# First two weight-block sums of 25 seven-product pairs: by DMAs that add in SBUF instead of one VectorE instruction each

## The chip, the cores and the metric

One core of a Trainium2 chip runs the whole kernel. The metric is the device time of one execution, in microseconds (us). The engines are named as in the profile: PE is TensorE's matmuls, PEld its weight loads, DVE is VectorE, ACT is ScalarE, POOL is GpSimd, and SP is SyncE, which here issues DMAs only (SPq is its queue).

## The reference

A decoder layer for 256 tokens of width 2048: a projection, two kinds of attention, an output projection with layer norm, and then the MLP, which is all that matters here:

```python
hdn = jnp.square(jax.nn.relu(jnp.einsum('bsd,df->bsf', x, w_ff1[l])))
ff_out = jnp.einsum('bsf,fd->bsd', hdn, w_ff2[l])
x = layer_norm(DEEPNORM_ALPHA * x + ff_out, ln2_g[l], ln2_b[l])
```

x is 256 x 2048, w_ff1 is 2048 x 8192 and w_ff2 is 8192 x 2048, all float32.

## The kernel before

**Three products for one.** Each float32 operand is split in a rounded part (hi, written by ScalarE as fp32r) and the rest (lo, written by VectorE as the difference). A product is then made as three matmuls: hi x hi, hi x lo, lo x hi (the helper `three`, L808 to L810).

**Parts and passes.** The 8192 hidden columns are worked in two parts, chunks 0 to 6 and 7 to 15 (`FF_PARTS`). In a part the hidden values of its chunks are made first (w_ff1). Then two passes over its rows of w_ff2 follow, one for each half (1024) of the output columns. So there are four passes: 0 and 1 from about 553 to 697 us, 2 and 3 from about 897 to 1082 us, with the hidden stage of part 1 between them.

**Pairs.** A pass goes over pairs of 128-row tiles of w_ff2, numbered through all passes as q (64 pairs; `PAIRS`). A pair's weights are a 2 x 2 grid of blocks of 128 x 512: tile t or t + 1, left or right 512 of the columns. There are two kinds. A plain pair (37 of them) makes the 8 block products of 2 tiles, 2 token halves and 2 column halves, 24 matmuls of 512 columns. A seven-product pair (27, `FAST`) makes 7 products, as in Strassen's and Winograd's scheme, 21 matmuls, from sums of weight blocks (`sum_raw`, four blocks) and from three of the blocks themselves ("own"), against sums of hidden blocks made earlier. The two kinds alternate, seven-product pair first, until the seven-product pairs of the pass are through; some plain pairs come at the end of a pass (3 in most). `NTH` counts the pairs of a kind.

**The steps of a seven-product pair q.** SyncE loads 1 MB into one of three buffers in two DMAs (`load_pair`, L490) once the pair that had the buffer before (q - 3) is split. VectorE makes the sums (`sum_pair`): first two blocks in one instruction of 1024 elements (L1640: block 1 + block 0 and block 2 + block 0), then the third from the first (L1647), then the fourth from the third (L1650), 512 each. ScalarE rounds the first two, then the last two (`round_sums`, L1188, L1190) and the own blocks (`round_own`, L1201). VectorE splits the first two, the last two (`split_sums`, L1659) and the own blocks (`split_own`, L1666). TensorE (`fast_group`) waits for the first split, multiplies with sums 0 and 1, then waits for the second and third split. sum_raw and sum_lo are one buffer; sum_raw, sum_hi and the own blocks exist once, so a step for the next pair waits until TensorE has used them (`fast_used`, counted three times in a pair).

**Plain pairs.** ScalarE rounds in two pieces of 1024 (L1181) and VectorE splits in two (L1631), in one of two homes.

**Order.** Each engine's order is written out by hand: pair after pair, for VectorE sums, splits, own, then the next plain pair. At the end of passes 0 and 2 (`end_pass`) it is: drain the low banks, sums of the next pass's first pair, split of the last plain pair, splits of those sums. GpSimd has no work in the passes: it waits for the final norm. The seven-product pairs 0 and 30 (`PART_END + 2`) are the first ones of each part; pair 30's sums are made before its part's plain pairs.

Of the kernel before, what the change touches and what calls it, by code (L numbers as in the profile page):

```python
# [4 lines left out]
P = 128  # L5
F32 = mybir.dt.float32
F32R = mybir.dt.float32r
ALU = mybir.AluOpType
ACT = mybir.ActivationFunctionType
# [9 lines left out]
NC = 512  # L19
CHUNKS = D_MODEL // NC  # L20
CHUNKS_FF = D_FF // NC
KU = 2
SLOTS = 4
UPH = KT // KU
# [4 lines left out]
U_FF1 = U_OUT + UPH * CHUNKS  # L29
# [44 lines left out]
HALF = D_MODEL // 2  # L74
# [18 lines left out]
PASSES = [(part, half) for part in range(2) for half in range(2)]  # L93
PAIRS = [(p, t) for p, (part, half) in enumerate(PASSES) for t, fast in pass_order(part, half)]
FAST = [fast for part, half in PASSES for t, fast in pass_order(part, half)]
PASS_START = [min(q for q, (of, t) in enumerate(PAIRS) if of == p) for p in range(len(PASSES))]
PASS_END = [max(q for q, (of, t) in enumerate(PAIRS) if of == p) + 1 for p in range(len(PASSES))]
NTH = [FAST[:q].count(FAST[q]) for q in range(len(PAIRS))]
FAST_END = [FAST[:end].count(True) for end in PASS_END]
PLAIN_END = [end - fast for end, fast in zip(PASS_END, FAST_END)]  # L100
PART_END = PASS_END[1]
# [10 lines left out]
STORE_ORDER = [0, 1, 2, 7, 3, 4, 5, 8]  # L112
BY_SCALAR = [6]

LAMBDA_INIT = 0.8 - 0.6
EPS = 1e-5
ALPHA = 2.0 ** 0.25
# [43 lines left out]
def hybrid_layer(nc, x, x_turned, w_in, lq1, lk1, lq2, lk2, subln_g, w_out, ln1_g, ln1_b, w_ff1, w_ff2,  # L161
# [3 lines left out]
    KB = 1024  # L165

    def at(name, shape, dtype, offset):
        return nc.alloc_sbuf_tensor_at(name, shape, dtype, offset=base + offset)
# [12 lines left out]
    X0 = 55 * KB  # L181
# [3 lines left out]
    H0 = X0 + 32 * KB  # L185
# [29 lines left out]
    E0 = H0 + 121 * KB  # L215
    sum_raw = at("sum_raw", [P, 4 * NC], F32, E0)
    sum_lo = at("sum_lo", [P, 4 * NC], F32R, E0)
    sum_hi = at("sum_hi", [P, 4 * NC], F32R, H0 + 97 * KB)
    last_hi = at("last_hi", [P, 4 * NC], F32R, X0 + 20 * KB)
    last_lo = at("last_lo", [P, 4 * NC], F32R, H0 + 16 * KB)  # L220
    last_raw = at("last_raw", [P, 4 * NC], F32, H0 + 24 * KB)
# [47 lines left out]
    def sem(name):  # L269
        sems[name] = nc.alloc_semaphore(name)  # L270
        return sems[name]
# [7 lines left out]
    w_rounded, w_split, w_used = sem("w_rounded"), sem("w_split"), sem("w_used")  # L279
# [26 lines left out]
    pair_loaded = [sem(f"pair_loaded{s}") for s in range(4)]  # L306
    plain_rounded, plain_split, plain_used = sem("plain_rounded"), sem("plain_split"), sem("plain_used")
    fast_summed, fast_rounded = sem("fast_summed"), sem("fast_rounded")
    fast_split, fast_used = sem("fast_split"), sem("fast_used")
    first_copied, mid_made, low_drained = sem("first_copied"), sem("mid_made"), sem("low_drained")  # L310
    y2_summed, tail_done, tail_summed = sem("y2_summed"), sem("tail_done"), sem("tail_summed")
# [12 lines left out]
    w_ff2_d = w_ff2.rearrange("l (t p) (h n) -> p (l t) h n", p=P, n=HALF)  # L324

    def ff1_raw(n):

        return n % SLOTS, (U_FF1 + n) // SLOTS

    def in_banks(c):  # L330

# [13 lines left out]
    def pair_raw(q):  # L345
        s = PAIR_SLOT[q]
        if s == 3:
            return last_raw[:, :]
        if s == 2:
            return more_raw[q > PART_END + 2][:, :]  # L350
        return w_raw[:, 2 * s:2 * s + 2, :].rearrange("p s n -> p (s n)")
# [118 lines left out]
    def load_pair(sp, q):  # L470

        p, t = PAIRS[q]
        part, half = PASSES[p]
        if q == 0:
            sp.wait_ge(w_used, U_FF1 + UPH)
        elif q == LAST:
            sp.wait_ge(fast_used, 3 * (FAST_END[2] + LAST_AFTER))
            sp.wait_ge(plain_used, PLAIN_END[2] + LAST_AFTER)
        elif q in (1, 2, PART_END, PART_END + 1):
            sp.wait_ge(w_split, U_FF1 + UPH * FF_PARTS[part][1] - (2 if q in (1, PART_END) else 0))  # L480
        elif q == PART_END + 2:
            sp.wait_ge(plain_split, 2 * PLAIN_END[1])
        elif q == PART_END + 5:
            sp.wait_ge(w_used, U_FF1 + UPH * CHUNKS_FF)
        elif FAST[q - 3]:
            sp.wait_ge(fast_split, 3 * (NTH[q - 3] + 1))
        else:
            sp.wait_ge(plain_split, 2 * (NTH[q - 3] + 1))
        for n in range(2):
            sp.dma_start(pair_raw(q)[:, n * HALF:(n + 1) * HALF],  # L490
                         w_ff2_d[:, t + n, half, :]).then_inc(pair_loaded[PAIR_SLOT[q]], 16)


    def tensor_program(pe):
# [466 lines left out]
    def scalar_program(act):  # L961
# [121 lines left out]
        for k in range(HALVED):  # L1083
            round_opening(k)
            for kk, (loaded, rounded) in enumerate(((half_loaded[k], half_rounded),
                                                    (w_loaded[k], w_rounded))):
                cols = slice(kk * NC, (kk + 1) * NC)
# [96 lines left out]
        def round_sums(q):  # L1184

            g = NTH[q]
            act.wait_ge(fast_summed, 3 * g + 1)
            act.activation(sum_hi[:, 0:2 * NC], sum_raw[:, 0:2 * NC], ACT.Copy).then_inc(fast_rounded, 1)  # L1188
            act.wait_ge(fast_summed, 3 * g + 3)
            act.activation(sum_hi[:, 2 * NC:4 * NC], sum_raw[:, 2 * NC:4 * NC], ACT.Copy).then_inc(  # L1190
                fast_rounded, 1)

# [85 lines left out]
        for n, i in enumerate(SCALED):  # L1278
            tt, cols = LAST_PIECES[i]
# [3 lines left out]
        for i in BY_SCALAR:  # L1283
            tt, cols = LAST_PIECES[i]
# [4 lines left out]
    def vector_program(dve):  # L1289
# [127 lines left out]
        for k in range(HALVED):  # L1417
            split_opening(k)
            for kk, (rounded, split) in enumerate(((half_rounded, half_split),
                                                   (w_rounded, w_split))):  # L1420
                cols = slice(kk * NC, (kk + 1) * NC)
# [78 lines left out]
        for n in range(OUT_END[0] - 1, UPH * (CHUNKS - 1)):  # L1500
            done = [c for c in range(CHUNKS - 1) if n == OUT_END[c] - 1]
# [131 lines left out]

        def sum_pair(q):

            g, raw = NTH[q], pair_raw(q)
            dve.wait_ge(pair_loaded[PAIR_SLOT[q]], 32 * PAIR_LAP[q])
            if g:
                dve.wait_ge(fast_used, 3 * g - 2)
            dve.tensor_tensor(sum_raw[:, 0:2 * NC].rearrange("p (b n) -> p b n", b=2),  # L1640
                              raw[:, NC:3 * NC].rearrange("p (b n) -> p b n", b=2),
                              raw[:, 0:NC].unsqueeze(1).to_broadcast([P, 2, NC]),
                              ALU.add).then_inc(fast_summed, 1)
            dve.wait_ge(fast_summed, 3 * g + 1)
            if g:
                dve.wait_ge(fast_used, 3 * g - 1)
            dve.tensor_tensor(sum_raw[:, 2 * NC:3 * NC], sum_raw[:, 0:NC], raw[:, 2 * NC:3 * NC],  # L1647
                              ALU.add).then_inc(fast_summed, 1)
            dve.wait_ge(fast_summed, 3 * g + 2)
            dve.tensor_tensor(sum_raw[:, 3 * NC:4 * NC], sum_raw[:, 2 * NC:3 * NC],  # L1650
                              raw[:, 3 * NC:4 * NC], ALU.add).then_inc(fast_summed, 1)

        def split_sums(q):

            g = NTH[q]
            for n in range(2):
                cols = slice(2 * n * NC, 2 * (n + 1) * NC)
                dve.wait_ge(fast_rounded, 3 * g + n + 1)
                dve.tensor_tensor(sum_lo[:, cols], sum_raw[:, cols], sum_hi[:, cols].bitcast(F32),  # L1659
                                  ALU.subtract).then_inc(fast_split, 1)  # L1660

        def split_own(q):

# [188 lines left out]
    def gpsimd_program(pool):  # L1852
        pool.wait_ge(powers_ready, 2)

        def rms_scale(h):


            pool.wait_ge(squared, h + 1)
            pool.tensor_tensor(mean_sq, sum_sq, eps_sum, ALU.add).then_inc(mean_ready, 1)
            pool.wait_ge(mean_ready, h + 1)  # L1860
            pool.tensor_tensor(root, mean_sq, minus_half, ALU.pow).then_inc(root_ready, 1)
            pool.wait_ge(root_ready, h + 1)
            pool.tensor_tensor(o_scale, root, inv_sums[h % 3][:, 0:4:2], ALU.mult).then_inc(scale_ready, 1)

        def norm_scale(norm):

            for tt in range(TT):
                n = TT * norm + tt + 1
                if norm == 0:
                    pool.wait_ge(moments, n)  # L1870
                    pool.tensor_scalar(var_eps[:, tt:tt + 1], mean_var[:, 2 * tt + 1:2 * tt + 2], EPS,
                                       None, ALU.add).then_inc(var_ready, 1)
                pool.wait_ge(var_ready, n)
                pool.tensor_tensor(inv_std[:, tt:tt + 1], var_eps[:, tt:tt + 1],
                                   minus_half[:, tt:tt + 1], ALU.pow).then_inc(std_ready, 1)


        pool.wait_ge(w_used, SLOTS + 1)
        pool.dma_start(ident_t[:, :], table[:, 0:P]).then_inc(ident_loaded, 16)
        for n, v in enumerate((lq1, lk1, lq2, lk2)):  # L1880
            pool.dma_start(lam_in[:, n, :], v.partition_broadcast(P).rearrange(
                "p l d -> p (l d)")).then_inc(lam_loaded, 16)
        pool.dma_start(subln, subln_g.rearrange("l d -> d l")).then_inc(lam_loaded, 16)
        pool.dma_start(tables[:, :], table[:, P:T_COLS]).then_inc(tables_loaded, 16)
        for h in range(N_DIFF):
            rms_scale(h)
        for n, v in enumerate((ln1_g, ln1_b)):

            pool.wait_ge(lam_summed, 2)
            pool.dma_start(ln1_gb[:, n, :], v.partition_broadcast(P).rearrange(  # L1890
                "p l d -> p (l d)")).then_inc(gb1_loaded, 16)
        norm_scale(0)

        norm_scale(1)

    with nc.Block() as block:
# [43 lines left out]
```

## Time and profile before

| | us |
|---|---|
| median of 3 runs | 1092.95 |
| range of the 3 runs | 1092.72 to 1093.32 |
| the profiled execution, its own time | 1093.56 |
| its span in the trace | 1091.5 |
| PE busy | 1086.6 (100% of the span) |
| DVE busy | 808.8 (74%) |
| ACT busy | 571.9 (52%) |
| POOL busy | 21.9 (2%) |

The span is what the trace holds; 2.1 us lie around it. A busy share is an average over the whole kernel and says nothing on which engine sets the end in a stage. For that the chain of waits is read, and the list of who waited for whom: an engine on which the end depends has no idle time, or has idle time that ends in another engine's event. Idle time of the others costs nothing. The start times that the timeline shows are us from the start of the span. A line of several instructions gives their time in sum, and matmuls overlap, so the distance of their starts is what one takes, not its length.

### The profile page before, as it was taken

Reading aid. Unit: us, or ns where it says so; the run is one execution under the profiler, and the core shown is the slowest. Engines: PE = TensorE matmul, PEld = TensorE weight load, DVE = VectorE, ACT = ScalarE, POOL = GpSimd, SP = SyncE. Lnnn points to the kernel's source line nnn. Section 1 sums busy time; section 2 is a strip of 40 time slices with the busy share of each in tenths; the row PEclk is TensorE's granted clock in tenths of the full one; section 3 lists DMA queues with packets and bytes.
Section 4 is the critical chain, followed back from the end, with each engine's and each line's share of the span. In section 5 each row is a group of like instructions: output and inputs, shape, how many; then the busy total and the mean of one; then the engine's idle time right before and its main releaser. Section 6 shows DMA issues by size and latency. Waiting matters only on the chain.

```text
span 1091.5 us, 13914 instructions
## 1 busy us (share of the span) xinstructions
PE 1086.6 (100%) x5611; PEld 922.7 (85%) x5611; DVE 808.8 (74%) x890; ACT 571.9 (52%) x723; POOL 21.9 (2%) x43
## 2 busy tenths in 40 slices
PE   9999999999999999999999999999999999999998
PEld 8888888888888888888888888888888888888886
DVE  6587857767656685667699898666676678889998
ACT  6487757665554524455455454344454455454561
POOL 1000000010000000000000000000000000000000
PEclk9999999999999999999999999999999999999999
DMA  9857565557555834665656556466656655656862
GB/s 302 258 176 223 183 192 154 174 165 252 166 171 162 284 113 155 193 189 178 215 190 223 199 195 227 163 191 192 193 174 200 215 182 194 230 195 192 284 216 78
DMA packets 108048, 213.83 MB, mean 196 GB/s; under 512 B 6785, under 2 KB 38017, under 8 KB 107473
## 3 DMA queue, kind: packets, MB, share of 16 engines
q1 hardware_dynamic: 107216, 209.61, 59.6%
q0 software_dynamic: 624, 3.21, 1.0%
q8 instruction: 44, 0.72, 0.3%
q14 instruction: 20, 0.16, 0.0%
q10 hardware_dynamic: 144, 0.13, 0.0%
HBM read 210.83 MB, written 2.10 MB: 195 GB/s over the span
## 4 chain that ended last, share of the span: by engine, by line
PE 98%; DVE 1%; DMA 0%; issue 0%; SPq 0%; ACT 0%; DVEq 0%
PE low_ps L790 11%; PE low_ps L629 10%; PE high_ps L790 10%; PE high_ps L810 8%; PE high_ps L808 8%; PE high_ps L809 8%; PE low_ps L522 6%; PE low_ps L526 6%; PE low_ps L524 6%; PE low_ps L795 5%; PE low_ps L634 5%; PE high_ps L795 5%; PE low_ps L810 2%; PE low_ps L808 2%; PE low_ps L809 2%; PE high_ps L569 1%
## 5 line engine op out<-in xcount | busy, mean ns | idle before, releaser
L1294 DVE TENSOR_TENSOR w_lo<-w_raw,w_hi 128x1024 fp32r<-128x1024 f32 x175 | 213.3, 1223 | 129.7 <-ACT w_hi L967 128.4
L967 ACT ACTIVATE w_hi<-w_raw 128x1024 fp32r<-128x1024 f32 x175 | 185.3, 1059 | 187.5 <-PE low_ps L526 67.9
L790 PE MATMUL low_ps<-x1T,w_hi 128*128 128x512 f32 x512 | 176.7, 393 | 0.0
L629 PE MATMUL low_ps<-xT,w_hi 128*128 128x512 f32 x448 | 156.8, 397 | 0.0
L790 PE MATMUL high_ps<-x1T,w_hi 128*128 128x512 f32 x448 | 155.0, 394 | 0.0
L795 PE MATMUL low_ps<-x1T,w_lo 128*128 128x256 f32 x512 | 136.9, 278 | 0.0
L1618 DVE TENSOR_TENSOR w_lo<-w_raw,w_hi 128x1024 fp32r<-128x1024 f32 x72 | 87.1, 1223 | 64.5 <-ACT w_hi L1166 64.5
L1166 ACT ACTIVATE w_hi<-w_raw 128x1024 fp32r<-128x1024 f32 x72 | 76.1, 1060 | 88.8 <-PE low_ps L790 43.4
L634 PE MATMUL low_ps<-xT,w_lo 128*128 128x256 f32 x448 | 122.3, 283 | 0.0
L795 PE MATMUL high_ps<-x1T,w_lo 128*128 128x256 f32 x448 | 119.8, 278 | 0.0
L809 PE MATMUL high_ps<-w_lo,hid 128*128 128x512 f32 x290 | 112.4, 388 | 0.0
L810 PE MATMUL high_ps<-w_hi,hid 128*128 128x512 f32 x290 | 112.4, 388 | 0.0
L808 PE MATMUL high_ps<-w_hi,hid 128*128 128x512 f32 x290 | 112.4, 388 | 0.0
L790 PEld LDWEIGHTS low_ps<-x1T,w_hi 128*128 128x128 f32 x512 | 94.3, 188 | 19.4
L795 PEld LDWEIGHTS low_ps<-x1T,w_lo 128*128 128x128 f32 x512 | 96.2, 188 | 2.8
L629 PEld LDWEIGHTS low_ps<-xT,w_hi 128*128 128x128 f32 x448 | 82.5, 188 | 17.4
L790 PEld LDWEIGHTS high_ps<-x1T,w_hi 128*128 128x128 f32 x448 | 82.6, 188 | 17.3
L634 PEld LDWEIGHTS low_ps<-xT,w_lo 128*128 128x128 f32 x448 | 84.6, 189 | 4.1 <-issue 1.7
L795 PEld LDWEIGHTS high_ps<-x1T,w_lo 128*128 128x128 f32 x448 | 84.2, 188 | 2.5
L1188 ACT ACTIVATE sum_hi<-sum_raw 128x1024 fp32r<-128x1024 f32 x27 | 28.6, 1060 | 102.1 <-DVE sum_raw L1640 102.1
L1659 DVE TENSOR_TENSOR sum_lo<-sum_raw,sum_hi 128x1024 fp32r<-128x1024 f32 x54 | 65.6, 1222 | 0.0
L809 PEld LDWEIGHTS high_ps<-w_lo,hid 128*128 128x128 f32 x290 | 54.4, 188 | 11.2
(216 smaller groups left out, 1913.4 us busy)
## 6 DMA issues: line engine op xcount, KB each, us to landing
w_raw<-in_w_ff SPq DMA_DIRECT2D x208, 512.0 KB, 4.3
w_raw<-in_w_in SPq DMA_DIRECT2D x93, 512.0 KB, 4.2
more_raw<-in_w_ff SPq DMA_DIRECT2D x42, 512.0 KB, 5.3
w_raw<-in_w_out SPq DMA_DIRECT2D x32, 512.0 KB, 3.8
x_raw<-in_x_turned SPq DMA_DIRECT2D x8, 256.0 KB, 5.7
y<-in_x SPq DMA_DIRECT2D x8, 256.0 KB, 4.7
side_raw<-in_w_ff SPq DMA_DIRECT2D x4, 512.0 KB, 6.9
w_raw<-in_w_in SPq DMA_DIRECT2D x6, 256.0 KB, 5.6
```

The costliest lines, as they stand in the source:

```text
L629: return pe.matmul(banks[:, b, :], w_hi[:, slot, cols], xT[:, t, :, :].rearrange("p h t -> p (h t)"), start=(t == 0), stop=(t == KT - 1))
L634: return pe.matmul(banks[:, b, 0:SEQ], w_lo[:, slot, cols], xT[:, t, 0, :], start=False, stop=False)
L790: return pe.matmul(banks[:, b, :], w_hi[:, slot, cols], x1T[:, t, :, :].rearrange("p h t -> p (h t)"), start=(t == 0), stop=(t == KT - 1))
L795: return pe.matmul(banks[:, b, 0:SEQ], w_lo[:, slot, cols], x1T[:, t, 0, :], start=False, stop=False)
L808: pe.matmul(acc, hi, right_hi, start=start, stop=False)
L809: pe.matmul(acc, hi, right_lo, start=False, stop=False)
L810: return pe.matmul(acc, lo, right_hi, start=False, stop=stop)
L967: act.activation(w_hi[:, slot, :], w_raw[:, slot, :], ACT.Copy).then_inc(w_rounded, units)
L1166: act.activation(w_hi[:, n % SLOTS, :], w_raw[:, slot, :], ACT.Copy).then_inc(w_rounded, 1)
L1294: dve.tensor_tensor(w_lo[:, slot, :], w_raw[:, slot, :], w_hi[:, slot, :].bitcast(F32), ALU.subtract).then_inc(w_split, units)
L1618: dve.tensor_tensor(w_lo[:, slot, :], w_raw[:, ff1_raw(n)[0], :], w_hi[:, slot, :].bitcast(F32), ALU.subtract).then_inc(w_split, 1)
L1659: dve.tensor_tensor(sum_lo[:, cols], sum_raw[:, cols], sum_hi[:, cols].bitcast(F32), ALU.subtract).then_inc(fast_split, 1)
```

## The change

For 25 of the 27 seven-product pairs (all but pairs 0 and 30; the list `QUEUED`), the first two sums aren't made by VectorE any more. SyncE loads the two blocks 1 and 2 of the pair once more, from HBM, as two DMAs of 256 KB into buffers of their own (`front0` and `front1` in part 0, the two halves of `front2` in part 1). When both have landed (`front_loaded`), GpSimd issues two DMAs of 256 KB that add block 0 from HBM into each of them (`accum_op=ALU.add`, `front_added`). ScalarE, VectorE's third sum and the first split read these buffers in place of sum_raw. In part 0 the first rounding and the first split are two instructions of 512 columns, since the buffers lie apart.

The front buffers exist once for each part. So SyncE waits, ahead of the loads for queued pair m, for the first split of queued pair m - 1. GpSimd runs through all 25 pairs in a loop of its own, ahead of its last norm step. The 1 MB load of each pair stays, block 0 and all.

```diff
+QUEUED = [q for q, fast in enumerate(FAST) if fast and q not in (0, PART_END + 2)]
+QUEUED_END = [sum(q < end for q in QUEUED) for end in PASS_END]
...
+def sums_until(q):
+
+    return sum(2 if n in QUEUED else 3 for n in range(q) if FAST[n])
...
+    front = [[at("front0", [P, NC], F32, H0 + 86 * KB), at("front1", [P, NC], F32, E0 + 8 * KB)],
+             [at("front2", [P, 2 * NC], F32, X0 + 28 * KB)]]
...
+        if q in QUEUED:
+            m = nth_queued(q)
+            if m:
+                sp.wait_ge(fast_split, 3 * NTH[QUEUED[m - 1]] + 1)
+            if m == QUEUED_END[1]:
+                sp.wait_ge(w_used, U_FF1 + UPH * CHUNKS_FF)
+            sp.dma_start(front_part(q, 0), w_ff2_d[:, t, half, NC:HALF]).then_inc(front_loaded, 16)
+            sp.dma_start(front_part(q, 1), w_ff2_d[:, t + 1, half, 0:NC]).then_inc(front_loaded, 16)
...
-            act.wait_ge(fast_summed, 3 * g + 1)
-            act.activation(sum_hi[:, 0:2 * NC], sum_raw[:, 0:2 * NC], ACT.Copy).then_inc(fast_rounded, 1)
-            act.wait_ge(fast_summed, 3 * g + 3)
+            if q in QUEUED:
+                act.wait_ge(front_added, 32 * (nth_queued(q) + 1))
+                act.wait_ge(fast_used, 3 * g - 2)
+                for raw, cols in front_spans(q):
+                    ins = act.activation(sum_hi[:, cols], raw, ACT.Copy)
+                ins.then_inc(fast_rounded, 1)
+            else:
+                act.wait_ge(fast_summed, sums_until(q) + 1)
+                act.activation(sum_hi[:, 0:2 * NC], sum_raw[:, 0:2 * NC], ACT.Copy).then_inc(fast_rounded, 1)
+            act.wait_ge(fast_summed, sums_until(q + 1))
...
             dve.wait_ge(pair_loaded[PAIR_SLOT[q]], 32 * PAIR_LAP[q])
-            if g:
-                dve.wait_ge(fast_used, 3 * g - 2)
-            dve.tensor_tensor(sum_raw[:, 0:2 * NC].rearrange("p (b n) -> p b n", b=2),
-                              raw[:, NC:3 * NC].rearrange("p (b n) -> p b n", b=2),
-                              raw[:, 0:NC].unsqueeze(1).to_broadcast([P, 2, NC]),
-                              ALU.add).then_inc(fast_summed, 1)
-            dve.wait_ge(fast_summed, 3 * g + 1)
+            if q in QUEUED:
+                dve.wait_ge(front_added, 32 * (nth_queued(q) + 1))
+                first = front_part(q, 0)
...
+            if q in QUEUED:
+                for raw, cols in front_spans(q):
+                    ins = dve.tensor_tensor(sum_lo[:, cols], raw, sum_hi[:, cols].bitcast(F32), ALU.subtract)
+                ins.then_inc(fast_split, 1)
...
+        for m, q in enumerate(QUEUED):
+            p, t = PAIRS[q]
+            half = PASSES[p][1]
+            pool.wait_ge(front_loaded, 32 * (m + 1))
+            for b in range(2):
+                pool.dma_start(front_part(q, b), w_ff2_d[:, t, half, 0:NC], accum_op=ALU.add).then_inc(
+                    front_added, 16)
```

## Rows read from the trace of the kernel before

**Rows 1.** The page: span, busy time, granted clock, chain that ended last.
```profile
span 1091.5 us, 13914 instructions
...
PE 1086.6 (100%) x5611; PEld 922.7 (85%) x5611; DVE 808.8 (74%) x890; ACT 571.9 (52%) x723; POOL 21.9 (2%) x43
...
PEclk9999999999999999999999999999999999999999
...
PE 98%; DVE 1%; DMA 0%; issue 0%; SPq 0%; ACT 0%; DVEq 0%
```

**Rows 2.** Waits, whole span: who waited for whom, us, times, longest.
```profile
PE low_ps L499 <- DVE zeros L1408: 1.0, 1, 1.0
PE low_ps L676 <- DVE w_lo L1423: 0.4, 1, 0.4
...
ACT sum_hi L1188 <- DVE sum_raw L1640: 102.1, 25, 9.4
```

**Rows 3.** Windows: length, PE, PEld, DVE, ACT, POOL busy, clock, DMA share, GB/s.
```profile
552.70:696.90 144.20, 144.20 (x638) 119.38 (x637) 127.13 (x122) 72.78 (x69) 0.00 (x0) 1.00 0.59 199
896.90:1072.00 175.10, 175.10 (x774) 145.01 (x773) 158.49 (x149) 91.92 (x87) 0.00 (x0) 1.00 0.62 210
```

**Rows 4.** Timeline, PE: first matmuls of pairs 2, 9, 10, 11 and 32.
```profile
562.88 0.39 PE L808 MATMUL low_ps<-sum_hi,hid 128*128 128x512 f32 x1
...
598.24 0.39 PE L808 MATMUL high_ps<-w_hi,hid 128*128 128x512 f32 x1
...
603.68 0.39 PE L808 MATMUL low_ps<-sum_hi,hid 128*128 128x512 f32 x1
...
608.44 0.39 PE L808 MATMUL high_ps<-w_hi,hid 128*128 128x512 f32 x1
...
917.72 0.39 PE L808 MATMUL low_ps<-sum_hi,hid 128*128 128x512 f32 x1
```

**Rows 5.** Timeline, DVE: pair 10, third sum, both sum splits, own split.
```profile
597.15 0.69 DVE L1647 TENSOR_TENSOR sum_raw<-sum_raw,w_raw 128x512 f32<-128x512 f32 x1 [0.56 <-PE high_ps L810]
...
598.49 2.44 DVE L1659 TENSOR_TENSOR sum_lo<-sum_raw,sum_hi 128x1024 fp32r<-128x1024 f32 x2
601.07 1.76 DVE L1666 TENSOR_TENSOR own_lo<-w_raw,own_hi 128x1536 fp32r<-128x1536 f32 x1
```

**Rows 6.** Timelines: first sums of pairs 2 and 38 (DVE), loads behind pair 32's (SP).
```profile
555.05 1.22 DVE L1640 TENSOR_TENSOR sum_raw<-w_raw 128x1024 f32<-128x1024 f32 x1
...
939.75 1.22 DVE L1640 TENSOR_TENSOR sum_raw<-w_raw 128x1024 f32<-128x1024 f32 x1 [0.21 <-PE low_ps L810]
...
901.23 0.90 SPq L490 DMA_DIRECT2D more_raw<-in_w_ff  x2
```

**Rows 7.** Line L490 (512 KB each), issues at 584 us; landings at 584, then 950.
```profile
L490 SPq DMA_DIRECT2D more_raw<-in_w_ff x2: 328/380/433, 584.1 to 584.5; - x2
...
DMA to landing us min/median/max: 4.5/4.9/5.3
...
DMA to landing us min/median/max: 5.0/6.0/6.9
```

**Rows 8.** DMA rate in 40 slices of the window 949.5 to 957.7 us.
```profile
GB/s 200 240 220 100 120 240 340 380 380 380 440 440 400 440 440 420 380 400 280 300 400 360 340 420 380 260 220 180 20 20 40 20 20 40 0 0 0 0 0 0
```

**Rows 9.** Line L384: the opening's 256 KB loads, and their landing.
```profile
L384 SPq DMA_DIRECT2D w_raw<-in_w_in x6: 421/432/432, 1.2 to 4.0; - x6
...
DMA to landing us min/median/max: 3.3/5.6/6.3
```

**Rows 10.** Line L1890: GpSimd's two 1024 KB loads, and their landing.
```profile
L1890 POOL DMA_DIRECT2D ln_gb<-in_ln_g x1: 662/662/662, 244.8 to 244.8; - x1
L1890 POOL DMA_DIRECT2D ln_gb<-in_ln_b x1: 535/535/535, 245.5 to 245.5; - x1
...
DMA to landing us min/median/max: 6.9/8.1/9.3
```

**Rows 11.** Window at the end of the span, columns as in rows 3.
```profile
1087.00:1091.00 4.00, 1.13 (x4) 0.68 (x4) 1.39 (x2) 1.09 (x3) 0.00 (x0) 1.00 0.75 262
```

## What I predict, and how it is worked out

> **What bounds the kernel now.** I read the page first: TensorE is busy 1086.6 of 1091.5 us at full clock and the chain that ended last is 98% PE [rows 1]. Then TensorE's own waits: two, 1.4 us in all, both in the opening [rows 2]. Then the stretches that the change touches, the four passes of the second feed-forward product: PE is busy 144.20 of 144.20 us and 175.10 of 175.10 us, VectorE (DVE) 127 and 158 [rows 3]. VectorE is the next busiest, but nothing of its 88 to 91% is waited for by TensorE. So there is no time to gain here; the question is what becomes late.
>
> How late may something be? One seven-product pair and one plain pair take TensorE 10.2 us: 4.76 us (603.68 to 608.44) and 5.44 us (598.24 to 603.68) [rows 4]. VectorE's splits of the front half of the sums of that pair end at 598.49 + 1.22 = 599.7, 4.0 us before TensorE starts on them at 603.68 [rows 4, 5]. With buffers as they are the lead doesn't grow beyond about 4 us: at 939.75 the sum waits for TensorE to let its buffer go [rows 6].
>
> **What is removed.** 25 of the 27 L1640 sums, 1.22 us each [rows 6]: 30 us of VectorE. TensorE didn't wait for VectorE, so this gives 0. ScalarE's long waits ahead of sum_hi (102.1 us in total) are slack too [rows 2]. The rest of VectorE's work stays: two single sums (0.69 each), the splits, the own blocks. The front rounding and the front split are cut in two pieces in the first two passes (some 0.15 us more per pair).
>
> **What is added: a ring.** front0/front1 (or front2) hold one pair. Per queued pair the following stand behind one another and none can start earlier, since the buffer is single and is let go by the front split (fast_split) of the queued pair before:
>
> (a) SyncE issues two 256 KB loads when that split is done, and the second lands. Two 512 KB loads issued back to back take 0.4 + 5.3 = 5.7 us until the second has landed (0.4 + 6.9 in a busier place) [rows 7]. Half the bytes at the 380 to 440 GB/s at which these bursts move [rows 8] are 1.4 us less: 4.3 us. Bounds: 0.4 + 3.3 = 3.7 us by the fastest 256 KB load of the kernel [rows 9], and 0.4 + 6.9 = 7.3 us if nothing is saved.
>
> (b) GpSimd wakes, issues two accumulating DMAs, and the second lands. The trace shows none that adds. The nearest rows are GpSimd's two 1024 KB loads: 0.66 and 0.54 us to issue, the first landed after 6.9 us, the second after 9.3 [rows 10]. Less 768 KB at about 380 GB/s (2.1 us) the first would be 4.8 us, the second lands one issue later: 5.5 us. The adding DMA must also fetch what is in the buffer, 512 KB more for the two, between nothing and 1.4 us: I take the middle, 6.2 us. Bounds: 3.3 + 0.6 = 3.9 us (as quick as the fastest plain 256 KB load), and 9.3 + 0.6 = 9.9 us.
>
> (c) ScalarE rounds while VectorE makes the two single sums, then VectorE splits: from 597.15 to 599.71 in the kernel before, 2.6 us, and 0.1 us for waking and the cut pieces: 2.7 us [rows 5].
>
> One turn is 4.3 + 6.2 + 2.7 = 13.2 us, against 10.2 us of TensorE. The ring sets the pace, and each turn is 3.0 us late.
>
> **Who stands behind the new waits.** On SyncE the wait for the front split stands ahead of the loads of the next, plain pair; those wait for the own split of the same earlier pair anyhow, which comes 3.1 us later (601.07 + 1.76 against 599.71) [rows 5], so it costs nothing. On VectorE and ScalarE everything of the pair and of the plain one after it stands behind front_added. GpSimd has nothing else until the final norm. TensorE, once it follows the ring, starts a pair when the front split is done, uses 2.0 us of work (nine products of 0.227) and then needs the own block, ready at 3.1: 1.1 us idle inside the pair, paid once per pass, since otherwise the ring hides it.
>
> **The sum, pass by pass.** The pairs in the ring are 5, 6, 6 and 8, so 4, 5, 5 and 7 turns.
> - Pass 0: VectorE reaches the first queued pair at 555.05 [rows 6]; split done at 557.75, TensorE wants it at 562.88 [rows 4]: a lead of 5.1. 4 x 3.0 - 5.1 = 6.9, and 1.1 for the own block: 8.0 us.
> - Turn to pass 1: the loads of the pair that opens it (pair 14) wait for the split of pair 11, 5.4 us after pair 10's front split (3.1 to the end of the own block and two plain splits, taken as about 1.2 us each like the other 1024-element steps). From there 0.8 (issues) + 4.3 + 6.2. VectorE stands at this pair's sums before it splits pair 13, which TensorE needs first. With pair 10's front split at 557.75 + 4 x 13.2 = 610.55: sums added at 627.25, two single sums, first half of pair 13 split at 629.9. TensorE finished pair 12 at 610.55 + 5.9 + 10.9 = 627.3. Stall 2.6 us. Pass 1 then starts with a lead of 3.0.
> - Pass 1: 5 x 3.0 - 3.0 + 1.1 = 13.1.
> - Pass 2: the first front loads go out at 901.2, behind the pair's own [rows 6]; split at 901.2 + 13.2 = 914.4, TensorE wants it at 917.72: lead 3.3. 15 - 3.3 + 1.1 = 12.8. Turn to pass 3: 2.6.
> - Pass 3: 7 x 3.0 - 3.0 + 1.1 = 19.1.
> Sum: 8.0 + 2.6 + 13.1 + 12.8 + 2.6 + 19.1 = 58.2 us. Against the profiled execution's own 1093.56 that is 1151.8; the median is 0.6 lower: 1151.2, say 1151 us.
>
> Bandwidth doesn't set the pace: a pair moves 2.1 MB now and 3.15 MB afterwards, 239 GB/s over 13.2 us, where bursts reach 380 to 440 [rows 8]. At 10.2 us it would be 309, still below.
>
> **A rule against the terms.** The Trainium skill, page "DMA: Bandwidth & Descriptors", section "Anatomy of one DMA — SWDGE (gpsimd) path", fits a DMA issued by GpSimd with about 2.0 us plus bytes over 436 GB/s. By it a 256 KB DMA is 2.6 us, an estimate, and two of them, the second issued 0.6 us later, some 3.8; the ring would be about 0.4 + 3.2 + 3.8 + 2.7 = 10.1 us and would cost nothing. The 1024 KB row contradicts it here, 6.9 us where the fit has 4.4 [rows 10], so I go by the rows; the case stands among the rivals.
>
> **Rivals.**
> 1. The ring fits under TensorE's period: not slower, about 1093 us. With both lower bounds a turn is 3.7 + 3.9 + 2.7 = 10.3 us, and the leads (about 3.9 per pass when TensorE sets the pace) hide it up to 10.2 + 3.9 / 7 = 10.8. For it: the 3.3 us landing. Against: every load of this stretch in [rows 7] took 4.5 us or more.
> 2. The adding DMA is much slower than a load: at the upper bounds 7.3 + 9.9 + 2.7 = 19.9 us a turn, 21 turns of 9.7 = 204, less 14 of leads, plus 4 of own blocks and some 12 at the turns of passes: about 1299 us. Halfway, at 16 us a turn, 21 x 5.8 - 14 + 4 + 9 = 121: 1214 us. For it: no row shows such a DMA. Against: the bytes are a quarter of those of [rows 10].
> 3. TensorE's clock falls to its lower level in the gaps that the ring opens (1.9 and 1.1 us of every 13.2). No row has the price of the lower level; at half rate for half of the work a pair would take TensorE 15.3 us, 2.1 more than the ring, in 21 turns 44 us on top: 1195 us; at half rate throughout 20.4 us, 151 on top: 1302 us. Against: from 1087 to 1091 us TensorE is busy 1.13 of 4 us and the granted clock stays 1.00 [rows 11]. The skill's page "TensorE: Matmul & The Clock Gate", section "Part 1: The HAM clock gate", says that idling brings the lower level back; the gaps of this forecast would have to be long enough for that.
>
> **Chances.** The ring between 11 and 16 us a turn, the forecast: 0.76. Ring fits: 0.09 (0.07 within 0.2%, 0.02 faster). Slow adding DMA, above 16 us: 0.10. Clock: 0.05. The low end of the range, 1105, is a ring of about 11.2 us (21 x 1.0 = 21, less 14 of leads, plus 5); the high end, 1214, one of 16. That leaves out rival 1, the shortest rings, and most of rival 2. A measurement of this kernel tells 0.2% (2.2 us) from no change: faster 0.02, same 0.07, slower 0.91. Faster has hardly a path, since TensorE has no idle time in the passes.
>
> **What would show it.** TensorE waits for sum_lo in the passes (now none), 20 to 60 us in total, and its busy share in the two stretches falls to 80 to 90%. VectorE idles for an adding DMA ahead of the first single sum (now L1647), once a pair; its busy time in all is 30 us less. Front splits of queued pairs lie 13.2 us apart (11 to 16). The landing of the front loads is near 4 us, of the adding DMAs near 5.5. The hidden stage between passes 1 and 2 keeps its length. If splits stay 10.2 us apart, step (b) was wrong; if PEclk falls in the passes, rival 3 is in play; if the pair's own loads (L490) land later than VectorE wants them, bandwidth was the bound after all.

## The result

The changed kernel takes 1248.68 us (median of 4 runs, 1246.27 to 1250.55) against 1093.01 us before: 1.1423 times as long, 95% interval 1.1401 to 1.1445. I had forecast slower, 1151 us with a range of 1105 to 1214. The way is right and the size is not: 156 us instead of 58.

The profiled execution took 1250.55 us and its span is 1248.7 us. Of the page, the lines that answer to [rows 1], and the two rows of the new DMAs (line, queue, number, size, median us from issue to landing):

```profile
span 1248.7 us, 14012 instructions
...
PE 1135.7 (91%) x5611; PEld 949.5 (76%) x5611; DVE 779.4 (62%) x876; ACT 572.0 (46%) x734; POOL 66.3 (5%) x93
...
PEclk9999999999999999998899779999999988998789
...
PE 61%; DMA 23%; DVE 8%; issue 5%; POOL 1%; SPq 1%; ACT 1%; DVEq 0%; ACTq 0%
...
front<-in_w_ff SPq DMA_DIRECT2D x50, 256.0 KB, 3.3
front<-in_w_ff POOLq DMA_DIRECT2D x50, 256.0 KB, 7.8
```

VectorE has 29 us less to do (808.8 to 779.4), as the change says. But the chain that ended last was 98% TensorE and is now 61%, with 23% in DMAs that write the front buffers. TensorE's waits, two in the opening before [rows 2], are now in the passes (who waited for whom, us in total, times, longest):

```profile
PE low_ps L844 <- DVE sum_lo L1708: 95.8, 21, 7.0
PE high_ps L844 <- DVE w_lo L1674: 9.7, 2, 4.9
PE low_ps L844 <- DVE own_lo L1722: 2.1, 3, 0.7
```

Twenty-one waits for the front split, as many as the turns of the ring that I had counted, but that is by chance: 19 of them end a turn, two stand at the first queued pairs of passes 0 and 2 (pairs 2 and 32), and the first turn of passes 1 and 3 ends in none. The two for w_lo are the turns to passes 1 and 3. The two stretches that cover the passes, with the columns of [rows 3]:

```profile
552.70:740.00 187.30, 142.11 (x545) 112.03 (x544) 97.78 (x106) 64.43 (x71) 18.75 (x22) 0.88 0.67 193
974.00:1230.00 256.00, 193.63 (x736) 152.92 (x735) 133.04 (x128) 85.12 (x81) 24.85 (x28) 0.87 0.65 190
```

TensorE is busy 76% of both, and the granted clock is no longer 1.00.

**One turn of the ring, read from the timeline.** Four queues in order (start, length, engine, line, what; in brackets the idle time before and who ended it):

```profile
580.98 0.33 SPq L526 DMA_DIRECT2D front<-in_w_ff  x1
...
584.03 3.47 SPq L518 DMA_DIRECT2D w_raw<-in_w_ff  x4
...
584.95 1.77 POOL L1955 DMA_DIRECT2D front<-in_w_ff  x2 [14.53 <-DMA front<-in_w_ff]
...
594.46 1.15 ACT L1227 ACTIVATE sum_hi<-front 128x512 fp32r<-128x512 f32 x2 [9.09 <-DMA front<-in_w_ff]
...
595.86 1.29 DVE L1708 TENSOR_TENSOR sum_lo<-front,sum_hi 128x512 fp32r<-128x512 f32 x2
...
597.17 0.33 SPq L526 DMA_DIRECT2D front<-in_w_ff  x1
597.54 0.43 SPq L527 DMA_DIRECT2D front<-in_w_ff  x1
```

SyncE issues at 580.98; the loads are there at 584.95: 4.0 us (I had 4.3). The adding DMAs are through at 594.46: 9.5 us (I had 6.2). Two single sums and the front split end at 597.15: 2.7 us (I had 2.7). The turn is 16.2 us instead of 13.2, and all of the error is in one of its three terms. The line at 584.03 is the next two pairs' own loads, 2 MB, issued just ahead of the adds.

At pair 14, which opens pass 1, the same DMAs have another price. Its adds run while SyncE has almost nothing to load:

```profile
645.67 1.80 POOL L1955 DMA_DIRECT2D front<-in_w_ff  x2 [24.41 <-DMA front<-in_w_ff]
...
651.44 1.15 ACT L1227 ACTIVATE sum_hi<-front 128x512 fp32r<-128x512 f32 x2 [5.31 <-DMA front<-in_w_ff]
```

That is 5.8 us. What differs is who shares the DMA engines. For the adds of 584.95, the window 588 to 594 us; for those of 645.67, the window 646.6 to 651 us (queue, packets, MB, share of 16 engines; q0 is GpSimd's queue, q1 SyncE's):

```profile
q1 hardware_dynamic: 374, 1.36, 58.1%
q0 software_dynamic: 287, 0.52, 47.7%
```

```profile
q0 software_dynamic: 286, 0.52, 73.1%
q1 hardware_dynamic: 14, 0.02, 1.3%
```

The same 0.52 MB, with 1.36 MB of pair loads beside it in the first and 0.02 MB in the second. In the first the two shares add up to over 100%: the engines are full. The pair loads come at this moment for a reason that stands in the code: VectorE's own split and the plain split, which release the next two 1 MB loads, follow the front split that started the ring's turn, by 3 and 5 us; the front loads take 4.

### The profile page after: what moved, and what is told of

It reads as the page before. It is cut to its first block, busy times and chain, and to the rows that moved or that the text cites. A ratio compares the mean times of both kernels' runs of the same rounds, so it can differ in the third digit from the quotient of the medians.

```text
span 1248.7 us, 14012 instructions
## 1 busy us (share of the span) xinstructions
PE 1135.7 (91%) x5611; PEld 949.5 (76%) x5611; DVE 779.4 (62%) x876; ACT 572.0 (46%) x734; POOL 66.3 (5%) x93
## 4 chain that ended last, share of the span: by engine, by line
PE 61%; DMA 23%; DVE 8%; issue 5%; POOL 1%; SPq 1%; ACT 1%; DVEq 0%; ACTq 0%
DMA front<-in_w_ff 23%; PE low_ps L826 9%; PE low_ps L665 8%; PE high_ps L826 8%; PE low_ps L558 5%; PE low_ps L562 5%; PE low_ps L560 5%; PE low_ps L831 5%; PE low_ps L670 4%; PE high_ps L831 4%; DVE sum_lo L1708 2%; DVE sum_raw L1696 1%; DVE sum_raw L1699 1%; DVE w_lo L1674 1%; POOL front L1955 1%
## 5 line engine op out<-in xcount | busy, mean ns | idle before, releaser
L1227 ACT ACTIVATE sum_hi<-front 128x512 fp32r<-128x512 f32 (+1 forms) x36 | 27.5, 791 | 266.0 <-DMA front<-in_w_ff 266.0
L844 PE MATMUL low_ps<-sum_hi,hid 128*128 128x512 f32 x81 | 45.5, 561 | 95.8 <-DVE sum_lo L1708 95.8
L844 PE MATMUL high_ps<-w_hi,hid 128*128 128x512 f32 x290 | 115.1, 397 | 9.7 <-DVE w_lo L1674 9.7
L846 PE MATMUL high_ps<-w_hi,hid 128*128 128x512 f32 x290 | 114.3, 394 | 0.0
L826 PEld LDWEIGHTS low_ps<-x1T,w_hi 128*128 128x128 f32 x512 | 94.3, 188 | 19.4
L844 PEld LDWEIGHTS low_ps<-sum_hi,hid 128*128 128x128 f32 x81 | 21.1, 261 | 108.6 <-DVE sum_lo L1708 55.3
L1696 DVE TENSOR_TENSOR sum_raw<-front,w_raw 128x512 f32<-128x512 f32 x17 | 11.8, 693 | 138.1 <-DMA front<-in_w_ff 110.9
L665 PEld LDWEIGHTS low_ps<-xT,w_hi 128*128 128x128 f32 x448 | 82.5, 188 | 17.4
```

The source lines that it names most:

```text
L665: return pe.matmul(banks[:, b, :], w_hi[:, slot, cols], xT[:, t, :, :].rearrange("p h t -> p (h t)"), start=(t == 0), stop=(t == KT - 1))
L826: return pe.matmul(banks[:, b, :], w_hi[:, slot, cols], x1T[:, t, :, :].rearrange("p h t -> p (h t)"), start=(t == 0), stop=(t == KT - 1))
L844: pe.matmul(acc, hi, right_hi, start=start, stop=False)
L846: return pe.matmul(acc, lo, right_hi, start=False, stop=stop)
```

## Experiments

Theory A: the ring of the single buffer sets the pace, and its turn is long because the adds share the DMA engines with the pair loads that the same splits release. Rivals: B, the adding is slow by itself, whatever runs beside it; C, the added traffic holds up TensorE; D, each pair summed by DMAs costs something wherever it stands.

### Pair loads held back until the adds are through

```diff
+        if q - 1 in QUEUED:
+            sp.wait_ge(front_added, 32 * (nth_queued(q - 1) + 1))
         for n in range(2):
             sp.dma_start(pair_raw(q)[:, n * HALF:(n + 1) * HALF],
```

> The changed kernel, but SyncE holds the 1 MB load of the plain pair behind each queued pair until that pair's two adding DMAs have landed, so that they have the DMA engines to themselves. Theory A (the adding DMAs take some 9.6 us instead of 5.8 because they share the DMA engines with 1 to 2 MB of pair loads released at the same moment): from the first issue to the second landing some 6 us, front splits 13 to 15 us apart instead of 16.3 to 19, some of the gain given back because front loads now queue behind two pairs' loads; about 1190 us. Rival B (9.6 us is what the adding DMAs take by themselves): they stay at 9 us or more and, as the pair loads now come later too, the time is 1250 us or more.

Measured 1228.39 us, 1.1234 times before (1.1215 to 1.1252). The same turn in this kernel:

```profile
575.01 0.33 SPq L528 DMA_DIRECT2D front<-in_w_ff  x1
...
582.08 1.77 POOL L1957 DMA_DIRECT2D front<-in_w_ff  x2 [13.65 <-DMA front<-in_w_ff]
...
587.58 1.15 ACT L1229 ACTIVATE sum_hi<-front 128x512 fp32r<-128x512 f32 x2 [6.31 <-DMA front<-in_w_ff]
```

The adds take 5.5 us instead of 9.5, and 5.5 to 5.9 us for 23 of the 25 pairs: B falls, and it is shown that the pair loads beside them make them long. But the front loads take 7.1 us instead of 4.0, since they now stand behind two pairs' loads. The turn is 15.3 us here and 16.1 us in the mean of the 21, where I expected 13 to 15. The collision is moved, not removed: a period has the same data to move whatever the order. I was too hopeful by 38 us.

### Copies in place of adds

```diff
-                pool.dma_start(front_part(q, b), w_ff2_d[:, t, half, 0:NC], accum_op=ALU.add).then_inc(
+                pool.dma_start(front_part(q, b), w_ff2_d[:, t, half, 0:NC]).then_inc(
```

> The changed kernel with GpSimd's 50 adding DMAs turned into plain copies of the same size from the same place: the sums are left out, all else stands. It prices the adding alone. Theory A: beside the pair loads a plain copy is slowed as well; the two adds held the engines about 3 us for 0.5 MB, where loads move 0.38 MB per us (1.4 us), so the turn is some 2 us shorter, 14 to 15 us, about 1205 us. Rival B (the adding is the slow part): the copies land after about 5.5 us, the turn is 12.5 to 13.5 us, about 1155 us, as I had forecast. Rival C (the adding costs nothing, issue by GpSimd and sharing cost all): same as the changed kernel, 1249 us.

This kernel leaves out the sums and serves only for its time. Measured 1199.65 us, ratio 1.0977 (1.0961 to 1.0993).

```profile
580.66 1.06 POOL L1955 DMA_DIRECT2D front<-in_w_ff  x2 [13.83 <-DMA front<-in_w_ff]
...
588.95 1.15 ACT L1227 ACTIVATE sum_hi<-front 128x512 fp32r<-128x512 f32 x2 [7.83 <-DMA front<-in_w_ff]
```

8.3 us where the adds took 9.5. GpSimd also issues two copies in 1.06 us and two adds in 1.77. So the adding is worth 1.2 us of this turn, 2.1 us of the mean turn (14.8 for 16.9 us), and 49 us of the whole. What the sharing is worth is seen at pair 14, where almost nothing runs beside the copies either; the second block is the window from 637.4 to 641.2 us:

```profile
636.91 1.06 POOL L1955 DMA_DIRECT2D front<-in_w_ff  x2 [24.80 <-DMA front<-in_w_ff]
...
641.22 1.15 ACT L1227 ACTIVATE sum_hi<-front 128x512 fp32r<-128x512 f32 x2 [6.05 <-DMA front<-in_w_ff]
```

```profile
q0 software_dynamic: 160, 0.52, 43.7%
q1 hardware_dynamic: 10, 0.03, 2.1%
```

Two copies take 4.3 us there, where the two adds took 5.8. So of the 9.5 us some 4.3 are two plain copies alone, 1.2 to 1.5 the adding, and the rest, 3.7 to 4.0, the sharing. The adds also move in 286 packets where the copies need 160.

### The traffic alone

In the kernel before, GpSimd loads and adds for 18 pairs into front buffers that nobody reads. A pair's loads go out after the front split of the seven-product pair before it, as in the change, but no engine of the passes waits for them:

```diff
+        for m, q in enumerate(FRONT):
+            pool.wait_ge(fast_split, 3 * NTH[q] - 2)
...
+            pool.dma_start(front_part(q, 0), w_ff2_d[:, t, half, NC:HALF]).then_inc(front_loaded, 16)
+            pool.dma_start(front_part(q, 1), w_ff2_d[:, t + 1, half, 0:NC]).then_inc(front_loaded, 16)
+            pool.wait_ge(front_loaded, 32 * (m + 1))
+            for b in range(2):
+                pool.dma_start(front_part(q, b), w_ff2_d[:, t, half, 0:NC], accum_op=ALU.add).then_inc(
+                    front_added, 16)
```

> The kernel before with the DMAs added and used by nobody: for 18 pairs GpSimd loads two 256 KB blocks and adds into them, one pair after another, at its own pace through the four passes; the sums are made by VectorE as before. Theory A (waits make the loss, not traffic): within 0.2% of the kernel before, 1093 us; the pair loads land somewhat later, which TensorE does not see. Rival C (the traffic itself holds up TensorE, by late pair loads or otherwise): 1105 us or more, with TensorE waiting for w_lo or sum_lo.

Measured 1094.24 us, ratio 1.0011 (1.0002 to 1.0021). In the windows of [rows 3]:

```profile
552.70:696.90 144.20, 144.20 (x637) 119.18 (x636) 127.12 (x122) 72.72 (x69) 21.60 (x30) 1.00 0.84 254
896.90:1072.00 175.10, 174.43 (x770) 144.12 (x769) 157.26 (x148) 91.97 (x87) 29.03 (x40) 1.00 0.87 269
```

The DMA engines are busy 84 and 87% instead of 59 and 62%, they move 254 and 269 GB/s, and TensorE idles for 0.7 us. C falls for this much traffic (72% of the change's): without the waits it costs 1 us.

### Every other pair

```diff
+QUEUED = QUEUED[::2]
```

> The changed kernel with only every second of the 25 pairs in the ring (13 pairs); the other 12 are summed by VectorE. The ring has two periods of TensorE, 20.4 us, for a turn of 16 to 19 us. Theory A (the single buffer's turn against TensorE's period makes the loss): the loss goes nearly altogether, 1093 to 1102 us, what is left coming from the first pair of each part, whose DMAs start late. Rival D (each pair summed by DMA costs something of its own, by waits or by traffic): 13/25 of 156 us stay, about 1174 us.

Measured 1163.46 us, ratio 1.0647 (1.0628 to 1.0666). This was a clear miss: the ring of the buffer has 20.4 us for its turn and should have cost next to nothing. 70 us for 13 pairs looks like rival D. The timeline of pair 16 shows the reason:

```profile
632.02 2.35 DVE L1675 TENSOR_TENSOR w_lo<-w_raw,w_hi 128x1024 fp32r<-128x1024 f32 x2
...
634.40 0.80 SPq L519 DMA_DIRECT2D w_raw<-in_w_ff  x2
635.25 0.43 SPq L527 DMA_DIRECT2D front<-in_w_ff  x1
...
641.64 1.77 POOL L1956 DMA_DIRECT2D front<-in_w_ff  x2 [36.79 <-DMA front<-in_w_ff]
...
650.80 1.15 ACT L1228 ACTIVATE sum_hi<-front 128x512 fp32r<-128x512 f32 x2 [14.33 <-DMA front<-in_w_ff]
...
653.53 0.80 PE L845 MATMUL low_ps<-sum_hi,hid 128*128 128x512 f32 x1 [4.23 <-DVE sum_lo L1709]
```

The front loads weren't waiting for the front buffer, which was free long before. They stand on SyncE's queue behind the pair's own 1 MB load, and that waits for a pair buffer, which VectorE frees at 634.37 by the split of pair 13. From there it is 0.9 us until they are issued, 6.4 us (behind 1 MB), 9.2 and 2.7 us: 19.1 us to the front split. Meanwhile VectorE stands at front_added with the next plain split behind it, which releases the next queued pair's load. So there is a second ring, theory E: where TensorE has two periods, 20.4 us, I put it at 24 to 26 us. Read over all nine turns within passes, the front splits lie 25.5 to 30.9 us apart, 27.1 in the mean; 9 times 6.7 us are 61 of the 70 us. I had named what stands behind the wait on VectorE, but hadn't closed this circle.

### Every other pair, front loads one pair earlier

```diff
         p, t = PAIRS[q]
         part, half = PASSES[p]
+        if q + 1 in QUEUED:
+            load_front(sp, q + 1)
```

`load_front` holds the three waits and loads of the change, taken from behind the pair's own load.

> As every_other (13 pairs in the ring, 1163 us), but SyncE issues a pair's two front loads one pair earlier, ahead of the 1 MB load of the plain pair before it, in place of behind the pair's own 1 MB load. Theory E (a second ring: front loads wait with the pair's own load for one of the three pair buffers, which the split of pair q - 3 frees; from there 19 us to the front split of q, and VectorE splits nothing else meanwhile): the front loads then go out about a front split of q - 4 earlier, 16 us are needed and 20.4 are there, so 1093 to 1098 us. Rival D (each pair summed by DMAs costs TensorE some 5 us wherever its DMAs are issued): 1163 us as before. Rival F (the adding DMAs are too slow beside the pair loads to fit at all): above 1130 us.

Measured 1092.95 us, ratio 0.9998 (0.9989 to 1.0008). All of TensorE's waits:

```profile
PE low_ps L544 <- DVE zeros L1460: 1.0, 1, 1.0
PE low_ps L853 <- DVE own_lo L1731: 0.5, 1, 0.5
```

The 70 us are gone by the place of two instructions on one queue. D falls: 13 pairs summed by DMAs cost nothing, though each of their adds still takes 7.6 us to land in the median. And the 15 us that VectorE has less to do (808.8 to 793.5) bring nothing. That the place on the queue made the loss is shown by this.

### Two front buffers in part 1

All 25 pairs, a second buffer (`front3`, 4 KB per partition) for passes 2 and 3, semaphores for each of two pairs in turn:

```diff
+             [at("front3", [P, 2 * NC], F32, X0 + 20 * KB)]]
...
+            back = 2 if m >= QUEUED_END[1] + 2 else 1
             if m:
-                sp.wait_ge(fast_split, 3 * NTH[QUEUED[m - 1]] + 1)
+                sp.wait_ge(fast_split, 3 * NTH[QUEUED[m - back]] + 1)
```

> The changed kernel, all 25 pairs, with a second front buffer in part 1 only (passes 2 and 3), so that the loads wait for the front split of the queued pair before the last. Of the 156 us lost, some 67 arise in part 0 and 90 in part 1. Theory A alone (one single-buffer ring): part 1's loss goes, about 1160 us. Theory E (behind it stands the second ring, through the pair buffers, 24 to 26 us for two pairs against 20.4): part 1 keeps some 2 to 2.7 us per pair, 25 to 30 us, so about 1185 us. Rival F (adding DMAs and loads together fill the DMA engines): front splits stay 14 us apart or more, above 1200 us.

Measured 1213.82 us, ratio 1.1100 (1.1083 to 1.1116). This is a miss: only 35 us of part 1's 90 come back, where theory E gave 60 to 65. The first ring alone (1160) is out. What I had written for rival F is met in its figures, above 1200 us and front splits about 14 us apart: 14.4 in pass 2, 13.8 in pass 3. Its cause isn't: in windows in these two passes the DMA engines are busy 75 and 87% (columns as in [rows 3]), and the next experiment moves the same data faster.

```profile
980.00:1054.00 74.00, 57.63 (x233) 45.84 (x231) 41.74 (x39) 29.27 (x28) 8.91 (x10) 0.91 0.75 213
1079.00:1167.00 88.00, 72.28 (x291) 58.26 (x290) 51.60 (x50) 30.47 (x29) 11.78 (x14) 0.91 0.87 269
```

In pass 2 a front split comes 25.7 to 27.8 us after the last but one before it, about the length that the second ring has in the kernel with every other pair. So I read it as E with a longer ring than the 24 to 26 us that I had worked with.

### Two front buffers, front loads one pair earlier, in part 1

```diff
+        if q + 1 in QUEUED and ((q + 1) > PART_END):
+            load_front(sp, q + 1)
```

> As two_buffers, and in part 1 the front loads are issued one pair earlier, ahead of the plain pair's 1 MB load. Theory E: both rings are open in part 1, its loss goes to 0 to 15 us, 1160 to 1175 us in all; what remains is part 0's. Rival F (DMA engines full: per pair 2.6 MB of loads at 0.38 MB per us and 3 us for the adds, 9.9 of 10.2 us): the front splits settle 11 us apart or more, 1180 us or above.

Measured 1168.42 us, ratio 1.0684 (1.0663 to 1.0706). From pair 30 to pair 60 TensorE takes 162.2 us, against 153.7 before, 241.3 in the changed kernel and 208.3 with two buffers alone: opening the second ring as well brings back 46 of the 55 us that were left. Window from 980 to 1100 us of this kernel:

```profile
980.00:1100.00 120.00, 116.14 (x510) 95.26 (x509) 89.14 (x85) 56.80 (x54) 19.61 (x22) 1.00 0.99 306
```

The DMA engines are busy 99%, at 306 GB/s, and the clock is back at 1.00. But the 8.5 us that remain aren't all bandwidth. By TensorE's first matmuls, 3.6 us arise up to pair 34 and 1.1 up to pair 36, and there one single-buffer wait is left in the code: `back` is still 1 for the second queued pair of part 1. Its front loads wait for the front split of the first (979.15), and since they now stand ahead of pair 33's own load on SyncE's queue, that waits too:

```profile
979.18 0.33 SPq L543 DMA_DIRECT2D front<-in_w_ff  x1
979.55 0.43 SPq L544 DMA_DIRECT2D front<-in_w_ff  x1
980.03 0.91 SPq L528 DMA_DIRECT2D more_raw<-in_w_ff  x2
```

The front split of pair 34 comes 17.6 us after that of pair 32. The other 3.8 us arise at pairs 54, 56 and 60, with the DMA engines full; the front splits of pass 3 lie 11.3 us apart, which is rival F's figure, while its time (1180 us or above) isn't reached. That bandwidth is the bound there is argued from the busy share; no run took traffic away at this pace.

### Both cures in one kernel

```diff
+QUEUED = QUEUED[:11:2] + QUEUED[11:]
```

with the two buffers in part 1 and the front loads one pair early in both parts.

> 20 of the 25 pairs by adding DMAs with both rings opened: in part 0 every other queued pair (6 of 11), in part 1 all 14 with two front buffers, front loads issued one pair early everywhere. Theories A and E together (lateness is the sum of what each part's rings are late, nothing else): part 0 0, part 1 the 8 to 9 us seen in two_buffers_early with the DMA engines full, so 1100 to 1103 us. If a cost per pair (rival D) is left, 1130 us or more. If the VectorE time that is taken off were worth anything, the time would be below 1093 us.

Measured 1101.95 us, ratio 1.0082 (1.0065 to 1.0099): inside the 1100 to 1103 us that the theory gave. Twenty pairs summed by DMAs cost 9 us. Of the 7.5 us between the spans, 4.5 arise at pairs 34 and 36 (917 to 942 us), where the second queued pair still waits for the buffer of the first and the DMA engines are full as well, and most of the rest from pair 54 on; from 980 to 1072 us the DMA engines are 0.95 busy. And the 23 us of VectorE's time that are saved (808.8 to 785.9) buy nothing. No version beat the kernel before.

## Why the prediction was wrong in size

- **What bounds the kernel: right.** TensorE, without idle time in the passes. VectorE's time was worth 0: shown by every_other_early, which takes 15 us of it off, isn't late, and has the time of before (ratio 0.9998).
- **The ring, its 21 turns, and its steps (a) and (c): right.** 4.0 us for 4.3 and 2.7 for 2.7 in the turn shown; 4.3 and 2.6 in the mean of the 21.
- **Step (b), the adding DMAs: this is the step that failed.** I took 6.2 us; they take 9.9 us in the mean of the 21 turns: 9.4 to 10.9 in 16 of them, 6.1 and 6.2 in the first turns of passes 1 and 3, and 12.0 to 12.4 in three. My working, from GpSimd's loads of [rows 10] less their bytes, comes near the price of the adds with the DMA engines to themselves: 5.8 us at pair 14, 5.5 us in the kernel that holds the pair loads back. In part that is luck: it had 5.5 us without the adding and 0.7 for it, where two plain copies alone take 4.3 and the adding 1.5. What it lacked is what runs beside it. I had compared the bytes of a whole turn with the burst rate and closed with "Bandwidth doesn't set the pace". That doesn't hold for the moment: the adds are issued just as the splits release up to 2 MB of loads. For the mean it holds at the traffic of traffic_only (254 and 269 GB/s, 1 us), but not at the 309 GB/s that I worked out for a period of 10.2 us and called "still below": with both rings open the DMA engines are 99% busy at 306 GB/s. My upper bound of 9.9 us is the measured mean; the turn of 16.9 us lies in rival 2, to which I gave 0.10, and a turn of 16 us was the edge of the range. The Trainium skill, page "DMA: Bandwidth & Descriptors", section "Queues, rings and completion order", says that a DMA engine takes turns between the queues that have work, packet by packet. The trace agrees as far as it goes: in the window of the slow adds both queues get on at once, with 374 and 287 packets. In what order the packets take turns, no row shows.
- **A turn of 16.2 us isn't the mean either.** Over the four passes the front splits of queued pairs lie 16.8, 16.6, 16.7 and 17.4 us apart, 16.9 over 21 turns. In two turns GpSimd's second add was issued 8.4 and 8.6 us after the first, with 7.6 us of idle time that no event in the trace ends, which makes those turns 18.7 and 19.0 us. I haven't tried what holds it.
- **The lead of pass 0: wrong.** I gave it 5.1 us; TensorE starts pair 2 at 564.7 instead of 562.9. Its front loads took 7.1 us behind two pairs' loads, and its adds 10.1.
- **The turns of passes: 9.6 and 9.8 us, not 3.7.** Pair 14's front loads, issued behind its own 1 MB, land after 7.75 us instead of 4.3, and TensorE waits 4.73 us for pair 13. It is the same kind of error, a DMA priced as if alone; here the load beside it stands ahead on the same queue.
- **The clock (rival 3): it fell, and it isn't what made the time.** Three windows around the gap before pair 8 (columns as in [rows 3]):

```profile
612.00:616.00 4.00, 0.35 (x1) 0.38 (x2) 3.08 (x5) 2.81 (x4) 0.00 (x0) 0.56 0.01 2
616.00:618.00 2.00, 2.00 (x6) 1.52 (x6) 1.85 (x2) 2.00 (x3) 0.00 (x0) 0.50 0.66 205
620.00:622.00 2.00, 2.00 (x10) 1.66 (x9) 0.83 (x1) 0.00 (x0) 1.27 (x2) 1.00 0.96 176
```

After TensorE idled for 6.9 us the granted clock is 0.50, the 1.2 GHz level, and the row has 6 matmuls at work in 2 us where there are 10 once the clock is back at 1.00, the 2.4 GHz level. [rows 11] had misled me: 1.00 there says nothing for longer gaps. The Trainium skill, page "TensorE: Matmul & The Clock Gate", section "Part 1: The HAM clock gate", has idling bring the lower level back, and the trace agrees. But in a turn of 16 us TensorE has 6 us to spare, and about 9 matmuls that start 0.43 instead of 0.23 us apart, 2 us, fit in. In 19 of the 21 turns TensorE waits for the front split at the end, for 2.95 us or more, so a faster clock would have made that wait longer and the turn no shorter. The clock can cost only where TensorE isn't waiting afterwards, at the turns of passes and in the tail; how much of their excess is its share, no run took apart.

The sum, in the form of the prediction, with what the trace of after has:

| term | forecast, us | measured, us |
|---|---|---|
| 21 turns beyond 10.2 us | 21 x 3.0 = 63.0 | 21 x 6.74 = 141.5 |
| leads at the four pass starts | -14.4 | -9.6 (1.85 and 0.78 us late in passes 0 and 2, 6.14 and 6.12 early in 1 and 3) |
| turns to passes 1 and 3, own block with them | 7.4 | 9.6 + 9.8 = 19.4 |
| ends of passes 1 and 3 | 2.2 | 3.0 + 2.9 = 5.9 |
| sum | 58.2 | 157.2 (spans: 157.2) |

The column on the right comes from TensorE's first matmuls, later than before by 1.9 us at pair 2, 28.2 at pair 10, 37.8 at 14, 63.6 at 24, 66.7 at 30, 67.4 at 32, 100.1 at 42, 109.9 at 46, 154.3 at 60 and 157.2 at the end, and from the front splits.

79 of the 99 us of error are the length of the turn, and the leads and pass turns come from the same kind of error, front loads and adds priced without what runs beside them.

The rule against the terms, the fit that the Trainium skill, page "DMA: Bandwidth & Descriptors", section "Anatomy of one DMA — SWDGE (gpsimd) path", has for a DMA issued by GpSimd, gave 3.8 us for two DMAs, an estimate. Two plain copies alone take 4.3 us here, so it is 0.5 us short for what it describes. It has no term for the adding (1.5 us more) and none for the pair loads beside (8.3 us for copies, 9.5 for adds). A ring that costs nothing, which followed from it, is refuted by the turn of 16.9 us.

## What to carry to other kernels

When work is moved from an engine to DMAs with a single buffer, write the turn of that buffer as a chain (wait, issue, landing, next issue, landing, use) and set it against the period of the engine that bounds the kernel; then price each DMA with what the same semaphores release at that moment, not alone and not by the mean rate. Follow also the queue that issues the loads: a load behind another one inherits its wait, and that can be a second, longer ring. Relief for an engine that nobody waits for is worth nothing, here 15 us and 23 us of it.

## What the runs showed of the hardware

Two adding DMAs of 256 KB from HBM into SBUF, from the first issue by GpSimd until the second has landed: 5.5 to 5.9 us with the DMA engines to themselves, 9.4 to 10.9 us in most turns beside pair loads (1.4 MB in the window shown). Two plain copies: 4.3 us alone, 8.3 us in the same place beside pair loads. The adds move in 286 packets, the copies of the same bytes in 160. GpSimd needs 0.9 us to issue an add, 0.5 us a copy. At 0.50 of the clock the 128 x 512 matmuls of this kernel start 0.43 us apart, at 1.00 they start 0.23 us apart; the first follow a gap of 6.9 us in the timeline:

```profile
615.65 0.76 PE L844 MATMUL low_ps<-sum_hi,hid 128*128 128x512 f32 x1 [6.90 <-DVE sum_lo L1708]
616.21 0.63 PE L845 MATMUL low_ps<-sum_lo,hid 128*128 128x512 f32 x1
616.64 0.63 PE L846 MATMUL low_ps<-sum_hi,hid 128*128 128x512 f32 x1
617.07 0.63 PE L844 MATMUL low_ps<-sum_hi,hid 128*128 128x512 f32 x1
```
